# Other places in the VectorE and ScalarE orders of a retention block: first weight lows, scaling of stored rows, split of the state, two steps of the samples

## The reference

```
o, s_new = retention(q, k, v, state)      # 4 heads, q/k 256 wide, v 512 wide
#   scores = (q k^T) * decay;  o = scores v + (decayed q) state
#   s_new  = decay * state + (decayed k)^T v
o = (o - mean(o)) * rsqrt(var(o) + EPS)   # per head
y_ret  = (o * gn_ret * silu(z_r)) @ w_branch_ret     # 2048 x 1024
y_pool = (pooled * silu(z_p)) @ w_branch_pool
x_out  = x + (sigmoid(gate_p) * y_pool + sigmoid(gate_r) * y_ret) @ w_out
y      = x_out * rsqrt(mean(x_out^2) + EPS) * g_final
```

## Time and profile before

| | |
|---|---|
| median of 3 runs | 2845.28 us (2842.68 to 2849.21) |
| the profiled execution | 2846.47 us, its span 2844.7 us |
| PE busy | 2794.3 us, 98% of the span |
| VectorE busy | 1808.9 us, 64% |
| ScalarE busy | 1127.4 us, 40% |
| DMA queue of SP | 541.73 MB, 53.3% of 16 engines' span |

### The profile page before, as it was taken

How to read it: one execution, slowest core, us unless ns; L and a number is a source line. 1 busy time by engine, 2 the same in 40 slices (tenths; PEclk the granted TensorE clock), 3 DMA queues, 4 the chain that set the end, 5 groups by cost and what they waited for, 6 DMA issues and landing times.

```text
span 2844.7 us, 36714 instructions
## 1 busy us (share of the span) xinstructions
PE 2794.3 (98%) x13504; PEld 2249.8 (79%) x13504; DVE 1808.9 (64%) x2588; ACT 1127.4 (40%) x1901; POOL 685.3 (24%) x456
## 2 busy tenths in 40 slices
PE   6999999999999999999999999999999999999998
PEld 5888888888877777777777787877887788778876
DVE  7657566667555365555666556776677667766775
ACT  5444444444564434443443433333333333333332
POOL 4343433435332233434343320000000000000000
PEclk9999999999999999999999999999999999999999
DMA  4544444454564344453544457477547754775496
GB/s 143 192 148 152 174 148 156 156 178 148 179 229 145 110 156 161 163 184 110 185 154 140 170 221 269 161 269 296 223 161 270 300 221 162 269 300 221 162 335 253
DMA packets 281849, 552.80 MB, mean 194 GB/s; under 512 B 24216, under 2 KB 166872, under 8 KB 270527
## 3 DMA queue, kind: packets, MB, share of 16 engines
q1 hardware_dynamic: 266279, 541.73, 53.3%
q10 hardware_dynamic: 15168, 8.46, 1.0%
q0 software_dynamic: 224, 0.26, 0.0%
HBM read 375.59 MB, written 175.14 MB: 194 GB/s over the span
## 4 chain that ended last, share of the span: by engine, by line
PE 92%; DVE 4%; issue 2%; DMA 1%; ACT 1%; POOL 1%; ACTq 0%; SPq 0%; DVEq 0%; POOLq 0%
PE bank L1310 29%; PE bank L1312 28%; PE bank L1311 28%; PE bank L1360 2%; PE bank L1383 1%; PE bank L1502 1%; DVE w_lo L2173 1%; PE bank L1632 1%; PE bank L1620 0%; PE bank L1610 0%; DVE xs L2187 0%; DMA raw<-in_w_branch_pool 0%; PE bank L1305 0%; DVE xa_lo L2173 0%; DMA x_d<-x_out 0%
## 5 line engine op out<-in xcount | busy, mean ns | idle before, releaser
L1310 PE MATMUL bank<-xa_hi,wa_hi 128*128 128x512 f32 x2240 | 889.3, 397 | 6.0 <-ACT part_s L1864 3.0
L1311 PE MATMUL bank<-xa_lo,wa_hi 128*128 128x512 f32 x2240 | 874.3, 390 | 0.0
L1312 PE MATMUL bank<-xa_hi,wa_lo 128*128 128x512 f32 x2240 | 874.1, 390 | 0.0
L1310 PEld LDWEIGHTS bank<-xa_hi,wa_hi 128*128 128x128 f32 x2240 | 421.0, 188 | 108.5 <-issue 22.7
L1312 PEld LDWEIGHTS bank<-xa_hi,wa_lo 128*128 128x128 f32 x2240 | 420.9, 188 | 90.1
L1311 PEld LDWEIGHTS bank<-xa_lo,wa_hi 128*128 128x128 f32 x2240 | 421.4, 188 | 83.0
L2173 DVE TENSOR_TENSOR wa_lo<-w_raw,wa_hi 128x512 fp32r<-128x512 f32 x320 | 312.9, 979 | 166.0 <-ACT wa_hi L1857 165.2
L2173 DVE TENSOR_TENSOR wa_lo<-w_sum,wa_hi 128x512 fp32r<-128x512 f32 x240 | 194.2, 809 | 241.1 <-ACT wa_hi L1857 241.1
L2173 DVE TENSOR_TENSOR w_lo<-raw,w_hi 128x512 fp32r<-128x512 f32 (+1 forms) x288 | 182.0, 659 | 193.2 <-ACT w_hi L1971 193.0
L1857 ACT ACTIVATE wa_hi<-w_raw 128x512 fp32r<-128x512 f32 x320 | 201.0, 628 | 242.6 <-PE bank L1312 238.3
L1971 ACT ACTIVATE w_hi<-raw 128x512 fp32r<-128x512 f32 (+1 forms) x288 | 166.9, 603 | 308.5 <-PE bank L1312 225.8
(11 more groups left out here) (253 smaller groups left out, 4318.3 us busy)
## 6 DMA issues: line engine op xcount, KB each, us to landing
w_raw<-in_w_in SPq DMA_DIRECT2D x80, 1024.0 KB, 5.4
v_d<-turned SPq DMA_DIRECT2D x64, 512.0 KB, 3.2
qk_s<-qk_d SPq DMA_DIRECT2D x32, 1024.0 KB, 7.7
v_s<-v_d SPq DMA_DIRECT2D x32, 1024.0 KB, 11.9
raw<-in_w_branch_ret SPq DMA_DIRECT2D x128, 256.0 KB, 4.4
tabs<-in_c_rope SPq DMA_DIRECT2D x16, 1024.0 KB, 7.0
qk_d<-high SPq DMA_DIRECT2D x32, 512.0 KB, 4.5
qk_d<-c_low SPq DMA_DIRECT2D x32, 512.0 KB, 5.4
```

What stands on the lines that cost most here:

```text
L1310: pe.matmul(out, lh, rh, start=first, stop=False, skip_group_check=onto)
L1311: pe.matmul(out, lh, rl, start=False, stop=False, skip_group_check=onto)
L1312: return pe.matmul(out, ll, rh, start=False, stop=last, skip_group_check=onto)
```

## The change

Five pieces of the written orders move. The work done is the same; the orders of PE, GpSimd and SP are the same.

1. Samples: the sixth state (index 5) is added ahead of the wait for z's sigmoid and of the product s_og, in each of four sample heads.
2. ScalarE, first head of blocks 1 to 3: the rounding of the state moves between that of the two scores.
3. VectorE, block 0: the lows of the first four units move from behind `output_bias(0, 1)` to one behind each z_lo of `gate_og(0)`.
4. VectorE, first head of blocks 1 to 3: the four scalings of the former block's rows, one run before, are placed one by one: tile 0 behind the first masked scores, tiles 1 and 2 behind their remainder, tile 3 behind the statistics. The state's remainder comes ahead of that of the second scores.
5. VectorE, the fourth piece of a sample head: the rotation comes ahead of the low instead of behind it.

```diff
@@ the names in the order of the samples' steps
-    "scale", "bias", "z_silu", "new5_0", "new5_1", "new6_0", "new6_1",
+    "scale", "bias", "new5_0", "new5_1", "z_silu", "new6_0", "new6_1",
@@ ScalarE, loop over b and h
-                    if h + 1 < HEADS:
+                    if b and h == 0:
+                        scores_high(hb + 1, 0)
+                        state_high(hb + 1, 0)
+                        scores_high(hb + 1, 1)
+                    elif h + 1 < HEADS:
                         scores_high(hb + 1, 0)
                         scores_high(hb + 1, 1)
@@ VectorE, gate_og(hb)
                     tt(z_lo[s][:, vt, :], z_in[s][:, vt, :], og_hi[:, vt, :].bitcast(F32), ALU.subtract, og_lo_done)
+                    if hb == 0:
+                        low(vt)
@@ VectorE, sample_head(h, n)
+                    new_sample_state(h, 5)
                     wait("head", h, "z_sig", s_act)
                     st(s_og[:], banks[3][:], s_og[:], ALU.mult)
-                    new_sample_state(h, 5)
@@ VectorE, last_lows(b, first, n)
+                    if k - BP0 == 3:
+                        sample_head(b, k - BP0)
                     low(b * UB + k + LEAD)
-                    sample_head(b, k - BP0)
+                    if k - BP0 != 3:
+                        sample_head(b, k - BP0)
@@ VectorE, loop over b and h
                     new_state(hb, 1)
-                    if b and h == 0:
-                        final(b - 1)
...
-                    if h + 1 < HEADS:
+                    if b and h == 0:
+                        mask_scores(hb + 1, 0)
+                        final(b - 1, (0,))
+                        scores_low(hb + 1, 0)
+                        final(b - 1, (1, 2))
+                        mask_scores(hb + 1, 1)
+                        state_low(hb + 1, 0)
+                        scores_low(hb + 1, 1)
+                    elif h + 1 < HEADS:
...
                     statistics(hb, 1)
+                    if b and h == 0:
+                        final(b - 1, (3,))
                     if h:
                         lows(b, (h - 1) * UH + 4, 1)
                     output_bias(hb, 1)
-                    if hb == 0:
-                        for u in range(RAW):
-                            low(u)
```

More of the change, by code:

```diff
@@ L2537, in out_variance, with final @@
                                          op0=ALU.mult, op1=ALU.add).then_inc(out_var, 1)
-            def final(b):
+            def final(b, tiles):
                 dve.wait_ge(out_pow, b + 1)
-                for i in range(NT):
+                for i in tiles:
                     dve.scalar_tensor_tensor(out=xo[:, i, :], in0=xo[:, i, :], scalar=out_inv[:, i:i + 1],
```

## The result

| | median us | runs |
|---|---|---|
| before | 2844.62 | 20 |
| after | 2849.51 (2847.01 to 2852.33) | 20 |

One of the 20 runs of before took 6114.65 us and is left out of the ratio. The ratio after to before is 1.0017, with a 95% interval of 1.0010 to 1.0024, which is +2.8 to +6.8 us. The forecast was 2848.7 as a median, +3.4 us on the profiled execution. The profiled execution of after took 2848.37 us, its span 2846.6.

What follows compares the result with a forecast made beforehand. PE is busy 98% of the span, but SP's in-order queue of loads also sets the time in each block's first half. 5.4 + 1.5 - 2.0 - 1.5 = +3.4 us, a median of 2848.7; range 2841.4 to 2855.

Steps and rivals of the forecast that it cites:

- C: Block 0's first lows: first half starts earlier, but SP's held loads make branch(0,1) +3.7 later, clock +1.7: +5.4 us.
- the bound of +7.1: Upper bound of C in block 0: +3.7 for the late loads plus 3.4 if the clock's fall lasts twice as long.
- D: Rows' scaling in pieces, blocks 1 to 3: st_lo wait of 0.97 goes, SP's later inputs give back more: +1.5 us.
- B: ScalarE's order in blocks 1 to 3, head 0: st_hi ahead of the second rounded scores; priced together with D, +1.5.
- the slack: Time from add_y's end to PE's second half in before: 5.3 us in block 1, 6.15 in block 3, block 2 alike.
- 3d - 5.3 - 2 x 6.15: Joint cost of blocks 1 to 3 at a delay d of head 2's inputs; +5 at 7.5, no block pays below 4.4.
- A: Samples' fifth state ahead of s_og and z's gate: PE's four waits on s_in go, -2.0 us.
- I name no loss: In A: s_og 1.28 later and its transposes after the states were given no cost.
- E: Last block, rotation before the low: the 2.3 wait for s_qk goes, PE soon meets the next limit: -1.5 us.
- The full gain: Rival: loads not binding, so the gains come whole, -13 together, 2832; chance 0.10.
- The held queue: Rival: SP behind tile 4's store in blocks 1 to 3 costs more; at delay 8, +8.3, 2853.6; chance 0.25.
- That the change would not bring st_lo forward: Rival in D: second mask and st_hi both wait for the second half's output; time within +3 to +4; chance 0.05.

Runs made afterwards that it cites:

- C alone: The kernel before with only the first lows of block 0 moved between the four z_lo: 2850.67 against 2845.14, ratio 1.0019.
- only the stores reordered: The changed kernel with SP in blocks 1 to 3 issuing head 2's inputs and units 5 to 8 ahead of tile 3's store: 2846.43 against 2844.67.
- parts 2 and 4 alone: The kernel before with only the scaling in pieces and ScalarE's and VectorE's order of the state: 2846.01 against 2844.67, ratio 1.0004.
- tile 3 later: The kernel before with parts 2 and 4, tile 3's scaling behind output_bias(hb, 1), SP's order untouched: 2851.57 against 2843.98, ratio 1.0025.
- only the first low put back: The changed kernel with the first of block 0's four lows back behind output_bias(0, 1): 2845.41 against 2845.14, ratio 0.9999.
- SP's orders alone: The kernel before with only SP's two reorderings, of block 0 and of blocks 1 to 3: 2843.00 against 2844.59, ratio 0.9996.
- SP's other orders: The changed kernel with both of SP's reorderings, of block 0 and of blocks 1 to 3: 2835.91 against 2844.67, ratio 0.9968.
- tile 3 in idle time: The changed kernel with both SP reorderings and tile 3 scaled in head 1 ahead of the lows of units 5 to 8: 2832.86 against 2843.98.

## Why the prediction was right, step by step

**C, +5.4 forecast, +5.56 measured.** The chain was as told: the first low ends at 1713.85, SP's load is issued at 1713.94, 3.94 us later than before when the passage is aligned (1713.94 - 1711.44 + 1.44), the burst moves as a whole, and the second half starts 3.79 later. The wait of 9.12 was told as 8 to 9, the clock's 1.77 as 1.7. One thing was left out: with the state early, PE's update ran into the next limit, the v rows of head 1, still on their way (0.89 us of wait in the run with C alone). It cost nothing, as the loads set the end.

That the size came out within 0.2 us is partly luck. The same passage cost 5.1 with C alone and 7.6 in the run with only the stores reordered, beyond the bound of +7.1. SP's load left 3.9 to 4.0 us late in all three, but from this load to the end of add_y it took 27.9, 27.35 and 28.9 us (27.75 in before), and the low clock cost 1.8, 1.8 and 2.8.

In before the granted clock fell behind waits of 1.5, 2.3 and 1.9 that follow one another; with parts 2 and 4 alone and tile 3 later it fell already behind the 2.3 of them (0.57 granted from 1712 to 1716). It fell behind 3.40 with only the first low put back and behind 1.77 in block 2 with tile 3 later, and not behind 1.62 in block 3 of that run. The Trainium skill ("TensorE: Matmul & The Clock Gate", section "HAM oscillation — how this bites in real kernels") puts the loss of clock on long gaps; on the wait of 9.12 the trace agrees, on the short ones the measurement decides, and they cost it too.

**D and B, +1.5 forecast, +1.06 measured, with two errors inside.** The wait for st_lo went, 0.97 to 1.15 a block, and head 2's inputs left 6.3 later, as worked out (1996.31 - 1986.39 = 9.92, less the 3.61 by which block 1 runs later). But the blocks were not sized right: +1.0, 0.25 and 0.25 were forecast, -0.12, +0.45 and +0.73 came. The term that failed is the slack. The prediction took the time from the inputs' issue to the end of add_y as fixed; it is 26.65, 25.67 and 25.84 in the three blocks of before, and 25.51, 26.21 and 26.54 in after, so a slack of 5.3 or 6.2 holds only to about 1 us (why it varies is not shown), and that the sum came out near is partly luck. Its own formula, 3d - 5.3 - 2 x 6.15, gives +1.3 at the delay of 6.3, not +1.5. And the working forgot that GpSimd's root would be late beside the scaling, which made the wait of 0.56; as the second half is set by the loads, this wait lies inside time that PE had to wait anyway. On the queue the trace bears out the rule of the Trainium skill ("DMA: Bandwidth & Descriptors", section "Anatomy of one DMA — SWDGE (gpsimd) path") that was weighed there: the wait is the issuing queue's, for head 2's inputs left right behind the last store's issue, and moving that one store behind units 5 to 8 took the three waits away.

**A, -2.0 forecast, -1.62 measured.** The four waits went, with a little more, 0.46 to 0.55 each. The term "I name no loss" was off by 0.42: PE waited once, in block 1, for the turned rows of the samples (s_ogt). The new order on VectorE is not what made them late, for the sixth state ends 22 us ahead of them. They stand right behind a low that waited for its weight:

```profile
2239.13 0.69 DVE L2177 TENSOR_TENSOR w_lo<-raw,w_hi 128x512 fp32r<-128x512 f32 x1 [1.27 <-ACT w_hi L1971]
2239.74 0.28 DVE L2552 TENSOR_TENSOR s_ogt<-bank,ret_g 128x128 f32<-128x128 f32 x1
```

The kernel with SP's orders alone, which keeps the old place of the states, has the same wait at the same matmul (0.23). So the wait hangs on when that weight comes.

**E, -1.5 forecast, -1.59 measured, and the agreement is luck.** In after 2.35 went, and 0.76 came back at the matmul of the pooled projection that the prediction had named, 10 us later. But the four kernels that keep the rotation at its old place lie 1.0, 1.4, 1.5 and 1.7 us below before in the same stretch (C alone, SP's orders alone, parts 2 and 4 alone, and these with tile 3 later), about as much as after (1.5 by this reading). The low ahead of the rotation had waited 4.19 us for its weight in the profiled execution of before, and 2.46 to 2.49 in these four. With parts 2 and 4 alone, VectorE's low and PE's wait:

```profile
2726.64 0.69 DVE L2177 TENSOR_TENSOR w_lo<-raw,w_hi 128x512 fp32r<-128x512 f32 x1 [2.47 <-ACT w_hi L1971]
...
PE bank L1597 <- DVE s_qk L2550: 0.8, 1, 0.8
```

So the term was sized by a wait that one execution had and four others had not. The nine kernels with the rotation moved gain 1.2 to 2.3 there, 1.8 on average, against the 1.4 that the four show on average; the rotation's own share is then some 0.4 us, and no run shows it by itself. Without E the steps of after sum to +5.0, beside the +4.9 of the medians.

**The rivals.** The full gain did not come, but the runs with SP's other orders show what its condition was: with loads that are not held it is -8.8, and -11.1 with tile 3 in idle time, near the 13 worked out for it (the steps of that trace, against the profiled execution that the 13 was read from, sum to -13.6). The held queue at a longer delay is the run with tile 3 later, +7.6 with parts 2 and 4 alone. That the change would not bring st_lo forward is refuted.

## What to carry to other kernels

Before an instruction is moved, look for the queue that waits for it, and count everything that stands behind that wait in order: here one low of 0.69 us held 23 us of transfers. A wait in a transfer queue belongs behind all that does not need it. A small operation of GpSimd on a chain needs a look at what VectorE does in the same microsecond. And a wait that is to be priced should be read in more than one profiled execution: the 2.3 us for s_qk were 0.3 to 1.4 in four others.

## What the hardware showed

A GpSimd operation of 0.70 us took 1.66 while VectorE ran a 1.28 us operation with both inputs in SBUF, and 0.70 beside one that read a PSUM bank; with the scaling moved away it took 0.70 in each of three further kernels. The kernel before had the same effect in its own trace: 12 of its 32 roots stand beside a low, whose inputs are two SBUF tiles, and take 1.07 or 0.80 instead of 0.70:

```profile
1743.37 0.68 DVE L2173 TENSOR_TENSOR w_lo<-raw,w_hi 128x512 fp32r<-128x512 f32 x1
...
1743.55 1.07 POOL L1265 TENSOR_TENSOR inv_std<-var_eps,half 128x2 f32<-128x2 f32 x1 [26.79 <-DVE var_eps L2442]
```

Beside an operation of 0.42, 0.69 or 1.28 us the root starts 0.17 or 0.18 behind it and ends 0.55 to 0.56 behind its end, in every trace of this case. So it is not slowed by a factor: it ends a fixed time behind VectorE's operation, however long that is. The Trainium skill ("SBUF — State Buffer", section "Who interferes with whom") says that a VectorE instruction with two SBUF inputs contends with a GpSimd instruction that reads SBUF, and that one with at most one such input, outside VectorE's two-port modes, does not; these rows agree with it.
